# Opening a two-layer block on one operand tile: first products, sums of squares and load order, and the last slot of a product by row half

## The reference

```
mod = silu(c) @ w_ada + b_ada                      # c: 2048, w_ada: 2048 x 6144
shift, scale, gate = split(mod, 3)
h = rms_norm(x, g_pre) * (1 + scale) + shift       # 256 x 2048
proj = h @ w_in                                    # 2048 x 20032
q_mla, kv_a, z_mla, qkv_dil, z_dil, gl_mla, gl_dil = split(proj)
a  = latent_attention(q_mla, kv_a) * silu(z_mla)
bb = dilated_attention(qkv_dil) * silu(z_dil)
x = x + gate * rms_norm((sigmoid(gl_mla) * (a @ w_mla) + sigmoid(gl_dil) * (bb @ w_dil)) @ w_o, g_post)
```

## Time and profile before

| what | value |
|---|---|
| median of 3 runs | 2448.31 us (2445.65 to 2450.62) |
| the profiled execution: its time, its span | 2449.69 us, 2448.3 us |
| TensorE busy (matmul) | 2371.4 us, 97% |
| VectorE, ScalarE, GpSimd busy | 1484.0, 1123.8, 117.2 us |
| mean DMA rate | 196 GB/s |
| first matmul of the opening's products | 27.80 us |

### The profile page before, as it was taken

One profiled execution on the slowest core, in us unless ns is written; L12 is line 12 of the kernel. 1 busy time (PEld: TensorE's weight loads), 2 busy tenths in 40 slices (PEclk: granted clock), 3 DMA queues, 4 the chain that ended last, 5 costly groups with the idle time before them and its releaser, 6 DMA issues.

```text
span 2448.3 us, 28030 instructions
## 1 busy us (share of the span) xinstructions
PE 2371.4 (97%) x11164; PEld 1963.0 (80%) x11164; DVE 1484.0 (61%) x2072; ACT 1123.8 (46%) x1472; POOL 117.2 (5%) x136
## 2 busy tenths in 40 slices
PE   7899999989999999999999999999999999999998
PEld 4567888878888898788888888888778878888777
DVE  6887565444445544677665676566655455465664
ACT  4233444534445454444344445554445555455443
POOL 1000000000000000000000100000100011010010
PEclk9999999989999999999999999999999999999999
DMA  9886544435553455888555644445665445545564
GB/s 357 320 317 245 161 137 146 159 111 188 183 190 116 149 183 200 308 289 280 178 182 180 202 148 171 166 161 180 220 201 189 173 172 172 175 162 180 184 221 172
DMA packets 135845, 478.94 MB, mean 196 GB/s; under 512 B 15793, under 2 KB 16049, under 8 KB 134689
## 3 DMA queue, kind: packets, MB, share of 16 engines
q1 hardware_dynamic: 130688, 458.42, 54.0%
q0 software_dynamic: 3728, 17.76, 2.0%
q10 hardware_dynamic: 1298, 0.97, 0.1%
HBM read 470.80 MB, written 6.29 MB: 195 GB/s over the span
## 4 chain that ended last, share of the span: by engine, by line
PE 80%; DVE 6%; ACT 3%; issue 1%; DMA 1%; DVEq 0%; ACTq 0%
PE G L470 24%; PE G L472 24%; PE G L471 24%; PE A L545 4%; DVE wlo L380 2%; PE A L794 1%; PE A L818 1%; ACT whi L378 1%; ACT dil L500 1%; PE A L994 1%; DMA raw<-in_weights 1%; DVE dil L1741 0%; PE A L1469 0%; DVE CP L1747 0%; PE A L960 0%
## 5 line engine op out<-in xcount | busy, mean ns | idle before, releaser
L380 DVE TENSOR_TENSOR wlo<-raw,whi 128x1024 fp32r<-128x1024 f32 (+2 forms) x774 | 926.6, 1201 | 729.1 <-ACT whi L378 726.7
L378 ACT ACTIVATE whi<-raw 128x1024 fp32r<-128x1024 f32 (+2 forms) x774 | 792.1, 1025 | 843.7 <-PE G L472 732.6
L470 PE MATMUL G<-whi,XH 128*128 128x512 f32 (+3 forms) x2804 | 1088.3, 388 | 20.5 <-DVE wlo L380 17.1
L472 PE MATMUL G<-whi,XL 128*128 128x512 f32 (+3 forms) x2804 | 1068.4, 381 | 0.0
L471 PE MATMUL G<-wlo,XH 128*128 128x512 f32 (+3 forms) x2804 | 1067.8, 381 | 0.0
L470 PEld LDWEIGHTS G<-whi,XH 128*128 128x128 f32 x2804 | 528.1, 188 | 122.0 <-DVE wlo L380 20.9
L472 PEld LDWEIGHTS G<-whi,XL 128*128 128x128 f32 x2804 | 527.3, 188 | 95.5
L471 PEld LDWEIGHTS G<-wlo,XH 128*128 128x128 f32 x2804 | 528.2, 188 | 90.1 <-issue 0.5
L330 DVE CUSTOM_DVE_ANT_0 raw<-raw,dil 128x1024 f32<-128x1024 f32 x64 | 84.9, 1340 | 10.5 <-DMA raw<-in_weights 10.5
L470 PE MATMUL A<-whi,XH 128*128 128x512 f32 x164 | 70.1, 427 | 6.6 <-DVE XL L646 3.4
L500 ACT ACTIVATE nat<-G 128x512 f32<-128x512 f32 (+4 forms) x102 | 51.2, 557 | 46.5 <-PE G L472 44.9
(11 more groups left out here) (198 smaller groups left out, 1599.3 us busy)
## 6 DMA issues: line engine op xcount, KB each, us to landing
raw<-in_weights SPq DMA_DIRECT2D x792, 512.0 KB, 4.2
raw<-in_weights SPq DMA_DIRECT2D x80, 384.0 KB, 3.0
raw<-in_weights SPq DMA_DIRECT2D x16, 288.0 KB, 2.8
spill<-nat POOLq DMA_DIRECT2D x8, 512.0 KB, 4.1
CP<-spill POOLq DMA_DIRECT2D x8, 512.0 KB, 4.7
raw<-in_weights SPq DMA_DIRECT2D x8, 336.0 KB, 3.1
FT<-in_xT SPq DMA_DIRECT2D x4, 512.0 KB, 5.8
Xn<-in_x POOLq DMA_DIRECT2D x1, 2048.0 KB, 11.8
```

What stands on the lines that cost most here:

```text
L378: th = AC.mark(nc.scalar.activation(h[:, 0:2 * cols], r[:, 0:2 * cols], ACT.Copy))
L380: tl = VE.mark(nc.vector.tensor_tensor(l[:, 0:2 * cols], r[:, 0:2 * cols], h[:, 0:2 * cols].bitcast(F32), ALU.subtract))
L470: nc.tensor.matmul(o, h, wh, start=(k == start), stop=False)
L472: ins = nc.tensor.matmul(o, l, wh, start=False, stop=(k == nkt - 1))
```

## The change

Four edits, shown in the diff.

- **Loads.** The first two modulation blocks are issued ahead of `x`. The first block of each of the first four products follows the first four modulation blocks, mixed with those of operand tile 1.
- **Sums of squares.** TensorE sums all 16 squared tiles into one bank, four matmuls after each part that ScalarE has squared; GpSimd's adds are gone.
- **First products.** Slots 0 to 3 are whole (`OPENING = 4`; two were). `open_products` multiplies operand tile 0 with all four of them, and then tile 1 with all four; tile 0 is made alone, ahead of the modulation blocks of tile 1.
- **Last slot by row half.** In the last slot of a product or of a group TensorE does both tiles for rows 0-127, marks that bank done, then both for rows 128-255. All evictions wait for their own bank's mark.

```diff
-WHOLE = frozenset([0, 1, *range(12, 22, 2), *range(24, 66, 4)])
+OPENING = 4
+WHOLE = frozenset([*range(OPENING), *range(12, 22, 2), *range(24, 66, 4)])
...
-    plan += modulation(0) + modulation(1)
+    second = modulation(1)
+    plan += modulation(0) + [first_slot(0), first_slot(1)] + second[:2] + [first_slot(2)] + second[2:] + [first_slot(3)]
...
-            for kk in range(2):
+            last = k0 + 2 == nkt
+            us = 3.45 if s in whole else 12 * (cols + 32) / 2400.0
+            for kk, hf in ((0, 0), (1, 0), (0, 1), (1, 1)) if last else ((0, 0), (0, 1), (1, 0), (1, 1)):
...
+                if last and (kk, hf) == (1, 0):
+                    PE.busy(us / 2)
+                    pair[0].done = PE.mark(ins)
-            PE.busy(3.45 if s in whole else 12 * (cols + 32) / 2400.0)
-            t = PE.mark(ins)
+            PE.busy(us / 2 if last else us)
+            t = pair[1].done = PE.mark(ins)
+            if not last:
+                pair[0].done = t
...
-                tk = act_copy(buf[:, hf, 0:cols], pair[hf].t[:, 0:cols], [t, free.get(key)], func, **kw)
+                tk = act_copy(buf[:, hf, 0:cols], pair[hf].t[:, 0:cols], [pair[hf].done, free.get(key)], func, **kw)
...
+        emit_loads(2)
         d_x = [load(SP, f"xt{n}", FT[:, 4 * n:4 * n + 4, :], i["xT"][:, 4 * n:4 * n + 4, :]) for n in range(4)]
...
+        def sum_of_squares(n):
+
             s4 = slice(4 * n, 4 * n + 4)
-            t_sq = act_copy(sqx[:, s4, :], FT[:, s4, :], [d_x[n]], ACT.Square)
-            if n:
-                GP.wait(t_sq, t_sum)
-                t_sum = GP.mark(nc.gpsimd.tensor_tensor(sqx[:, 0:4, :], sqx[:, 0:4, :], sqx[:, s4, :], ALU.add))
-            else:
-                t_sum = t_sq
+            PE.wait(act_copy(sqx[:, s4, :], FT[:, s4, :], [d_x[n]], ACT.Square))
+            for k in range(4 * n, 4 * n + 4):
+                ins = nc.tensor.matmul(G[3].t[:, 0:T], ones[:, :], sqx[:, k, :], start=(k == 0), stop=(k == KT - 1))
+            return PE.mark(ins)
...
-        emit_splits(-1)
-        operand_rows(*GROUPS[0])
+        operand_rows(0, 1)
+        emit_splits(OPENING - 1)
+        operand_rows(1, 2)
...
+        def open_products():
+
+            for kk in range(2):
+                PE.wait(whole_ready[kk])
+                for x, n in enumerate(STARTED[:OPENING]):
+                    pair = pair_for(0, n)
+                    if kk == 0:
+                        PE.wait(pair[0].free, pair[1].free, loaded[wslots[x]])
+                    for hf in range(2):
+                        ins = nc.tensor.matmul(pair[hf].t[:, :], FT[:, kk, hf * 128:(hf + 1) * 128],
+                                               in_raw(wslots[x])[:, kk * 512:(kk + 1) * 512],
+                                               start=(kk == 0), stop=(kk == 1 and n not in RESIDENT))
+                        PE.busy(0.86)
+                        if kk == 1:
+                            pair[hf].done = mm_done[x] = PE.mark(ins)
+                    if kk == 1:
+                        raw_free[wslots[x]] = [mm_done[x]]
+                        emit_loads()
```

More of the change, by code:

```diff
@@ L114, in weight_plan @@
         later = sum((modulation(j) for j in range(nlo, nhi)), [])
-        slots = [("w", "w_in", opened[n][1], 512, k) for n in STARTED for k in range(lo, hi, 2)]
+        slots = [("w", "w_in", opened[n][1], 512, k) for n in STARTED[0 if g else OPENING:] for k in range(lo, hi, 2)]
         for n, slot in enumerate(slots):
@@ L232, in __init__ @@
         self.t = t
+        self.done = None
         self.free = []
@@ L506, in to_nat @@
                 for hf in range(2):
-                    VE.wait(t, free.get(key))
+                    VE.wait(pair[hf].done, free.get(key))
                     toks.append(VE.mark(nc.vector.tensor_tensor(buf[:, hf, 0:cols], pair[hf].t[:, 0:cols],
@@ L593, in first_and_second_block @@
         t_cs = []
-        t_sum = None
         for n in range(4):
@@ L702, in first_and_second_block @@
                 if n in RESIDENT:
-                    pair = first[RESIDENT.index(n)]
-                    if g == 0:
-                        PE.wait(pair[0].free, pair[1].free)
-                    for k0 in range(lo, hi, 2):
[L707 to L713, removed]
+                    if g:
+                        for k0 in range(lo, hi, 2):
+                            gemm_slot(pair_for(g, n), 512, k0, KT, XH, XL, ready)
+                    continue
+                pair = pair_for(g, n)
+                e = PARTIAL.index(n)
+                if g or n not in STARTED[:OPENING]:
+                    PE.wait(pair[0].free, pair[1].free)
+                    for k0 in range(lo, hi, 2):
+                        gemm_slot(pair, 512, k0, hi, XH, XL, ready, lo)
                 for hf in range(2):
@@ L1281, in first_and_second_block @@
                 dst = GL[0][:, hf, 512 * c:512 * c + 512]
-                VE.wait(t, *gl_t[0][c])
+                VE.wait(pair[hf].done, *gl_t[0][c])
                 tk = VE.mark(nc.vector.tensor_tensor(dst, pair[hf].t[:, :], dst, ALU.mult))
@@ L1330, in first_and_second_block @@
                 d1 = GL[1][:, hf, 512 * c:512 * c + 512]
-                VE.wait(t, *gl_t[1][c])
+                VE.wait(pair[hf].done, *gl_t[1][c])
                 tk = VE.mark(nc.vector.tensor_tensor(d1, pair[hf].t[:, :], d1, ALU.mult))
@@ L1346, in first_and_second_block @@
                 dst = OUTn[:, hf, 512 * c:512 * c + 512]
-                ts = act_copy(sq[:, :], pair[hf].t[:, :], [t, free.get("sq")], ACT.Square,
+                ts = act_copy(sq[:, :], pair[hf].t[:, :], [pair[hf].done, free.get("sq")], ACT.Square,
                               accum_out=small[:, 4 * hf + c:4 * hf + c + 1])
@@ L1580, in layer_norm @@
                     d = Xn[:, hf, 512 * c:512 * c + 512]
-                    VE.wait(t)
+                    VE.wait(pair[hf].done)
                     tk = VE.mark(nc.vector.scalar_tensor_tensor(out=d, in0=d, scalar=ALPHA, in1=pair[hf].t[:, :],
```

49 lines of the change are left out of this document (29 added, 20 removed).

## The result

The changed kernel takes 2433.49 us (median of 5 runs, 2427.49 to 2434.59) against 2447.56 us of the kernel before (5 runs, 2445.18 to 2450.62): the ratio is 0.9937, with a 95% interval of 0.9926 to 0.9949, so by the ratio it is 15 us faster (the medians lie 14.1 apart). I had said 2440.7 us, 7.6 us faster, and 2435.5 at the least. The profiled execution is the 2433.49 one, with a span of 2432.0 us.

A forecast was written before the change was run, and what follows sets the result against it. TensorE, busy 97% of the span, was taken as the bound, gains lying in its waits: -2.4 + 0.4 for the start, -5.9 for row halves, 0.3 taken back, so 2448.31 would become 2440.7 us (8 in 10: 2435.5 to 2447).

The forecast's parts named there:

- the split waits: TensorE's 14 waits for splits, 17.1 us in all: earlier evictions would save 0 to 5 us, taken as -1.0.
- the exchanges: About 17 splits or copies trading places in the written order behind the opening: 0.3 us of the gain taken back.
- Rival 3: Each of eleven exchanges outside the busy stretch becomes a wait of 1.2 us: slower, 2453.9 us; chance 0.07.
- the dry ring: Weight queue dry for 6 us from 28.5 us: 0.4 us lost, 2 if landing is 1.6 slower.
- The opening term: Start of the kernel: fifth product 2.4 us earlier, less 0.4 for the weight queue running dry.
- The steps up to 40 us: Sums end at 19.0 us, first product at 23.7, tile 0 done at 33.0, tile 1 at 39.9, fifth product at 40.2.
- the last output: End of the kernel: one eviction and two operations remain behind the last pass instead of two and four, -1.4 us.
- the first layer's end: TensorE's 3.56 us stop at 1831.49 us, the same chain as at the kernel's end: -1.4 us.
- the normalisation: The normalisation whose wait is 1.3 us: one ScalarE square fewer behind the last pass, -0.7 us.
- the two waits for XL: Two layer norms that wait 0.4 us each for XL: -0.8 us if nothing else is late.
- The 0.6 for the groups' `kept`: Groups 1 to 3: TensorE waits 3.2 us for `kept` twice; half an eviction pair saved, -0.6 us.
- Rivals 1 and 2: Rival 1 (0.16): sums stay slow or ring not caught up, 2444.4 us; rival 2 (0.17): row halves hidden, 2444.9 us.

The follow-up runs named there:

- e4: The changed kernel with early evictions kept, but the planner reckoning with the whole slot's end, so VectorE's and ScalarE's order is the old one; 2431.12 us.
- e1: The new opening alone, with row halves, evictions and the order behind the opening as in the kernel before; 2447.58 us, ratio 0.9994 to the kernel before.
- e3: The changed kernel, but both evictions wait for the slot's end, with the old order on VectorE and ScalarE; 2445.69 us.
- e2: The kernel before with its old opening, plus the row halves, early evictions and the planner's exchanges; 2433.93 us, ratio 0.9938 to the kernel before.
- e12_three: e4 with three products opened on the first tile instead of four, the fourth split as before; 2430.87 us.
- e10_gates: e4 with the planner's new due times only in the first layer's gates and outputs (930 to 1840 us); 2430.12 us.
- e14_shift1: e10_gates with five extra passes of 512 columns in front of one product at some 385 us; 2435.23 us.
- e9_notail: The changed kernel, but with the old due times in the second layer, undoing the exchanges there; 2433.06 us.

## Why the prediction was wrong

The direction was right, and every place that gained more than 0.5 us was on the list; two terms were too small by more than the rest together.

**The step that failed: the split waits**, "few begin with an eviction; 0 to -5, I take -1.0". At the 14 places the sum went from 17.1 to 9.8 us, -7.3. Of this, -2.4 is the place at 980 us, which waits for its block and differs from execution to execution; the earlier trace rows shows one execution, and the price of that wait could not be read from it. At the other places it is -4.9. With the written order kept (e4) -2.4 of it remains: 1.0 at 1645 us, 1.0 at 1367 and 0.4 at 230, so the term was too small by 1.4, within its bounds. I looked for evictions directly ahead of the splits on VectorE; at 1645 and 1367 the evictions stand on ScalarE, ahead of the operand's or the block's rounding, and GpSimd's rotation behind them slows VectorE. The other -2.5 is the exchanges' (0.9 at 255, 0.75 at 1410, 0.6 at 2250, 0.2 at 1367).

**The second: the exchanges**, to which I gave +0.3. They were worth -3.5 at full clock (e4 to the changed kernel), in spite of one new wait of 1.4. As I read the written orders, work that the planner lets go half a slot earlier went ahead of a split for which there was time, or a split itself was written earlier; place by place this is not tested. Rival 3, that each becomes a wait, was wrong at all but one place.

**The third, on the other side: the dry ring**, 0.4 taken, 2 as its bound. The fifth product came 2.9 us earlier and group 1's scaling 1.1: 1.8 us were lost, near the bound. The opening term, -2.0, is -0.2 (e1) to -1.2 (e3) at full clock, 0.4 more against the kernel before of their own set. The steps up to 40 us held to within 0.9 us in the profiled execution, but what counted was the queue behind them.

**Right in size:** the last output (-1.3 for -1.4), the first layer's end (-1.1 for -1.4), the normalisation (-0.7), the two waits for XL (-0.8). Not listed by me: 0.5 us where the heads' stage evicts into nat (1.3 to 0.8). The 0.6 for the groups' `kept` came under another name: those waits are 3.2 as before, but the operand tile built behind the last `kept` of its group (XL, by L646 and L664) is waited for 1.83 us at 103.57 before and 1.24 at 101.81 after. (Two slots of 8 x 0.43 instead of 12 x 0.223 are 1.5 us more of TensorE, not the 1.4 of the working; the sum does not use it.)

**The sum, corrected,** at full clock: -0.2 to -1.2 for the opening, -9.3 for the early evictions, -3.5 for the exchanges, together -13.0 to -14.0, against -14.0 (2430.7 to 2416.7). In the waits that I can name, the early evictions come to -7.4 of the -9.3 (2.4 for splits, 1.3, 1.1, 0.7, 0.8, 0.5 and 0.6); where the rest comes from is not shown, the place at 980 us being one candidate. The three are steps of one chain of kernels, so that they must add up where e3 stands for the opening; the test is e2, which has the last two without the first: -13.8, against -12.8. The clock, of which I counted nothing, gave the changed kernel 1 to 2 us more, which lies within what the clock varies between runs. Rivals 1 and 2 both had a true part (the start gives little; the waits are set later in a chain), but the chain was the one that the halves shorten.

What stays open: what the early evictions do to the wait at 980 us, whether the exchanges of the second layer cost anything, and why the clock falls in that stretch in most executions of a kernel and not in others.

## What to carry to other kernels

To price an earlier eviction, follow what hangs on it through every queue up to the next wait of TensorE, even when that wait bears another name, and through the engine that works beside it: here five of the fourteen microseconds were listed under the weight splits. Look in a second profile whether a wait stands before pricing it; the longest of these differed by 1.2 us between two executions of one program. When a front is brought forward, ask which buffers it holds longer; a product opened early on a whole block kept the ring's buffer, and the queue was dry. Split a difference of under 1% into time at full clock and time lost to the clock before explaining it; the second can hide the first (e12_three) or add half of it again (e4_old_due).

## What the runs showed of the hardware

I had not expected the clock's share to hang on so little. Kernels of one written order lost 9.3 us to it (e10_gates) or 13.6 (e14_shift1, five passes more), and one kernel (e9_notail) ran at 2426.84 or at 2433, with a mean clock of 0.997 or 0.994; where it ran at 2426.84, its profile shows no fall at 476 to 515 us. The longest wait of TensorE there is 3.2 us. The Trainium skill ("TensorE: Matmul & The Clock Gate", on a second failure mode, psum-queue depth-cycling) describes such falls for a kernel in which TensorE idles briefly and often between groups of matmuls. The traces agree that a stretch of many short waits (TensorE busy 6.04 of 10 us) can lose the clock, and add that the same stretch can keep it.

Two more things show in the timelines. VectorE's split of a block takes 1.21 us by itself and up to 2.18 beside GpSimd's rotation. And where the weights' queue runs at some 415 GB/s, as ahead of 980 us, the wait for the next block is 1.8 us in one execution and 2.95 in another of the same program.
